# Group norm behind a scan: an earlier bonus load, gate products among the gains, scale and addition in PSUM, four products behind the spreads

## What the reference computes

```python
seq_first = lambda t: jnp.swapaxes(t, 0, 1)
s0 = jnp.zeros((B, H, N, N), f32)
_, y = lax.scan(step, s0, (seq_first(rh), seq_first(wh), seq_first(kh),
                           seq_first(vh), seq_first(kk), seq_first(bh)))
y = jnp.swapaxes(y, 0, 1)
mean = jnp.mean(y, axis=-1, keepdims=True)
var = jnp.mean(jnp.square(y - mean), axis=-1, keepdims=True)
y = ((y - mean) * lax.rsqrt(var + GN_EPS) * ln_w.reshape(H, N).astype(f32)
     + ln_b.reshape(H, N).astype(f32))
bonus = jnp.sum(rh * kh * r_k.astype(f32), axis=-1, keepdims=True) * vh
y = (y + bonus).reshape(B, S, RW_WIDTH).astype(h.dtype)
return (y * jax.nn.silu(gate)) @ w_out
```

## Time and profile before

| | us |
|---|---|
| median of 3 runs (lowest, highest) | 1218.44 (1214.68, 1219.96) |
| profiled execution, its own time | 1217.13 |
| its span, first to last instruction | 1215.3 |
| TensorE busy | 1155.3 (95%) |
| VectorE busy | 742.9 (61%) |
| ScalarE busy | 616.6 (51%) |
| GpSimd busy | 460.8 (38%) |

### The profile page before, as it was taken

How to read it: one execution, slowest core, us unless ns; L and a number is a source line. 1 busy time by engine, 2 the same in 40 slices (tenths; PEclk the granted TensorE clock), 3 DMA queues, 4 the chain that set the end, 5 groups by cost and what they waited for, 6 DMA issues and landing times.

```text
span 1215.3 us, 19475 instructions
## 1 busy us (share of the span) xinstructions
PE 1155.3 (95%) x7562; PEld 891.6 (73%) x7562; DVE 742.9 (61%) x1184; ACT 616.6 (51%) x1028; POOL 460.8 (38%) x375
## 2 busy tenths in 40 slices
PE   6999999989987999899999989999999999999997
PEld 5656777768955777677777767787888888777666
DVE  7758997846666345666676473472394234567764
ACT  6766546425753456455665554452212344566655
POOL 1431023456722444332333334443454445432321
PEclk9998999999998999899999999999999999999988
DMA  9812436253072443222222123432333333321111
GB/s 299 235 52 61 105 86 217 88 161 81 11 262 76 149 131 87 69 59 64 70 70 69 54 71 91 153 103 70 102 89 104 90 101 97 93 71 53 52 35 70
DMA packets 199373, 121.59 MB, mean 100 GB/s; under 512 B 27821, under 2 KB 187254, under 8 KB 198902
## 3 DMA queue, kind: packets, MB, share of 16 engines
q1 hardware_dynamic: 196822, 118.09, 33.2%
q10 hardware_dynamic: 2464, 2.29, 0.6%
HBM read 104.11 MB, written 16.25 MB: 99 GB/s over the span
## 4 chain that ended last, share of the span: by engine, by line
PE 44%; issue 29%; POOL 13%; DVE 9%; ACT 2%; DMA 1%; SPq 0%; POOLq 0%; ACTq 0%; DVEq 0%
POOL b_w_lo L612 13%; PE banks L695 11%; PE banks L697 11%; PE banks L696 11%; PE banks L702 1%; PE banks L1290 1%; PE banks L943 1%; DVE b_suffix L2681 1%; PE banks L1318 1%; DVE b_a_lo L2055 1%; DVE b_w_lo L2165 1%; PE banks L962 1%; PE banks L1300 1%; PE banks L1009 1%; PE banks L1034 1%
## 5 line engine op out<-in xcount | busy, mean ns | idle before, releaser
L612 POOL TENSOR_TENSOR b_w_lo<-b_w_raw,b_w_hi 128x512 fp32r<-128x512 f32 x304 | 404.7, 1353 | 705.8 <-ACT b_w_hi L1388 705.7
L695 PE MATMUL banks<-b_a_lo,b_w_hi 128*128 128x512 f32 x1264 | 517.7, 410 | 23.8 <-DVE b_a_lo L2336 10.5
L697 PE MATMUL banks<-b_a_hi,b_w_lo 128*128 128x512 f32 x1264 | 498.6, 394 | 0.0
L696 PE MATMUL banks<-b_a_hi,b_w_hi 128*128 128x512 f32 x1264 | 497.3, 393 | 0.0
L695 PEld LDWEIGHTS banks<-b_a_lo,b_w_hi 128*128 128x128 f32 x1264 | 240.3, 190 | 103.0 <-issue 21.4
L1388 ACT ACTIVATE b_w_hi<-b_w_raw 128x1024 fp32r<-128x1024 f32 x160 | 168.9, 1056 | 252.0 <-PE banks L697 240.7
L697 PEld LDWEIGHTS banks<-b_a_hi,b_w_lo 128*128 128x128 f32 x1264 | 240.0, 190 | 52.8
L696 PEld LDWEIGHTS banks<-b_a_hi,b_w_hi 128*128 128x128 f32 x1264 | 240.9, 191 | 43.9
L1804 ACT ACTIVATE b_exps<-banks,b_stats 128x128 f32<-128x128 f32 (+3 forms) x64 | 33.2, 524 | 61.1 <-DVE b_stats L2471 61.1
L1720 ACT ACTIVATE b_a_hi<-b_x_t,b_params 128x512 fp32r<-128x512 f32 x48 | 33.9, 718 | 54.7 <-DVE b_x_t L2344 54.2
L2344 DVE TENSOR_TENSOR b_x_t<-b_x_t,banks 128x512 f32<-128x512 f32 x32 | 22.0, 686 | 60.8 <-PE banks L697 60.8
(11 more groups left out here) (330 smaller groups left out, 1520.4 us busy)
## 6 DMA issues: line engine op xcount, KB each, us to landing
b_w_raw<-rw_w_in SPq DMA_DIRECT2D x32, 512.0 KB, 4.4
b_w_raw<-da_w_in SPq DMA_DIRECT2D x32, 512.0 KB, 4.1
b_w_raw<-w_in_a SPq DMA_DIRECT2D x32, 512.0 KB, 4.0
b_w_raw<-pe_w_gate SPq DMA_DIRECT2D x16, 512.0 KB, 4.1
d_ple<-b_ple_out SPq DMA_DIRECT2D x16, 256.0 KB, 3.4
b_w_raw<-rw_w_out SPq DMA_DIRECT2D x8, 512.0 KB, 4.1
b_ple_in<-d_ple SPq DMA_DIRECT2D x2, 2048.0 KB, 11.3
b_w_raw<-da_w_out SPq DMA_DIRECT2D x8, 512.0 KB, 3.9
```

What stands on the lines that cost most here:

```text
L612: m = pool.tensor_tensor(WLO[:, u % 2, ks], WRAW[:, u, ks], WHI[:, u % 2, ks].bitcast(F32), ALU.subtract)
L695: pe.matmul(dst, hi, a_lo[:, k_act, :], start=first, stop=False)
L696: pe.matmul(dst, hi, a_hi[:, k_act, :], start=False, stop=False)
L697: return pe.matmul(dst, lo, a_hi[:, k_act, :], start=False, stop=last)
```

## The change

- The bonus tiles' load moves ahead of the load of x, and the tiles lie where the squares lay, and the other way round (the new place is free once the load of L545 may start). The spread table's load stays where it is.
- The first four head sums move behind the last centring.
- Embeddings 4 and 5 move, with 6 and 7, behind the spreads: embedding j ahead of spread j for j from 4 on. Spreads 4 to 7 wait for the low part j - 4 (`act_ready`), since the bank now holds the value until then.
- ScalarE rounds the spread table ahead of its wait for the head sums; its copies of embeddings and weights are moved to fit.
- VectorE makes gate products 0, 1 and 2 behind gains 1, 3 and 5, with the wait for `gn_in` (both loads) behind gain 1; 3 to 5 ahead of the combination, 6 behind it, 7 in the loop.
- Scale and addition write the spread's bank; ScalarE and VectorE split from there.

```diff
-    BVT, SPREADH2, SPREADHR2, RK2, RKS2, RKC2 = phase([
-        ("bonus_v", [P, NT, TOK]), ("spread_heads2", [P, 2, P]), ("spread_heads2_r", [P, 2, P], F32R),
+    GSQ, SPREADH2, SPREADHR2, RK2, RKS2, RKC2 = phase([
+        ("gn_squares", [P, NT, TOK]), ("spread_heads2", [P, 2, P]), ("spread_heads2_r", [P, 2, P], F32R),
         ("gn_rstd", [P, TOK]), ("gn_signed", [P, TOK], F32R), ("gn_parts", [P, TOK], F32R)])
-    (GSQ,) = phase([("gn_squares", [P, NT, TOK])], 2 * FULL)
+    (BVT,) = phase([("bonus_v", [P, NT, TOK])], 2 * FULL)
...
         sp.dma_start(P1[:, :, :, :].bitcast(F32), D_P1).then_inc(sem("p_spilled"), 16)
+        sp.dma_start(BVT[:, :, :], D_BV.rearrange("j p t -> p j t")).then_inc(sem("gn_in"), 16)
         sp.wait_ge(sem("v_placed"), 2 * 2 * NC)
         sp.dma_start(XT[:, :, :], D_XT.rearrange("j p t -> p j t")).then_inc(sem("x_spilled"), 16)
         sp.wait_ge(sem("y_even"), 2 * NC)
         sp.wait_ge(sem("y_odd"), 2 * NC)
-        sp.dma_start(BVT[:, :, :], D_BV.rearrange("j p t -> p j t")).then_inc(sem("gn_in"), 16)
         sp.dma_start(SPREADH2[:, :, :], a["spread_heads"]).then_inc(sem("gn_in"), 16)
...
             if j == NT - 1:
-                gn_sums(0)
                 pe.wait_ge(sem("gn_kept"), 1)
...
-        gn_sums(1)
+        for b in range(2):
+            gn_sums(b)
         pe.wait_ge(sem("gn_kept"), NT)
-        for n in range(2, 6):
-            second_embedding(n)
+        second_embedding(2)
+        second_embedding(3)
         pe.wait_ge(sem("gn_rstd"), 2)
         for j in range(NT):
-            if j >= 6:
+            if j >= 4:
+
                 second_embedding(j)
-            if j >= 4:
-                pe.wait_ge(sem("gn_scaled"), j - 3)
+                pe.wait_ge(sem("act_ready"), A_RWO + j - 3)
             head_spread(BANK[4 + j % 4], SPREADHR2, RKC2, j).then_inc(sem("gn_bcast"), 1)
...
+        act.wait_ge(sem("gn_in"), 32)
+        act.activation(SPREADHR2[:, :, :], SPREADH2[:, :, :], ACT.Copy)
         act.wait_ge(sem("gn_mm"), 2)
...
-        act.wait_ge(sem("gn_in"), 32)
-        act.activation(SPREADHR2[:, :, :], SPREADH2[:, :, :], ACT.Copy)
...
         keep_second(2)
+        hi(RUN_RWO[0])
         keep_second(3)
-        hi(RUN_RWO[0])
-        keep_second(4)
-        keep_second(5)
         for k in range(NT):
             act.wait_ge(sem("gn_done"), k + 1)
-            split(0, k, YT[:, k, :])
-            if k == 1:
-                keep_second(6)
-            if k == 2:
-                keep_second(7)
+            split(0, k, BANK[4 + k % 4])
+            if k < 4:
+                keep_second(4 + k)
+            if k == 4:
                 hi(RUN_RWO[0] + 1)
...
             stt(out=YT[:, j, :], in0=gn_bank(j), scalar=prm(LN_W, j), in1=GT[:, j, :], op0=ALU.mult, op1=ALU.mult
                 ).then_inc(sem("gn_kept"), 1)
-
-        def gated_bonus(j):
-            own.step(stt(out=BVT[:, j, :], in0=BVT[:, j, :], scalar=prm(LN_B, j), in1=GT[:, j, :], op0=ALU.add, op1=ALU.mult))
+            if j == 1:
+                dve.wait_ge(sem("gn_in"), 32)
+            if j in (1, 3, 5):
+                gated_bonus(j // 2)
...
-            tt(YT[:, j, :], YT[:, j, :], BANK[4 + j % 4], ALU.mult).then_inc(sem("gn_scaled"), 1)
+            tt(BANK[4 + j % 4], YT[:, j, :], BANK[4 + j % 4], ALU.mult).then_inc(sem("gn_scaled"), 1)
...
-            tt(YT[:, j, :], YT[:, j, :], BVT[:, j, :], ALU.add).then_inc(sem("gn_done"), 1)
-
-        dve.wait_ge(sem("gn_in"), 32)
-        for j in range(4):
+            tt(BANK[4 + j % 4], BANK[4 + j % 4], BVT[:, j, :], ALU.add).then_inc(sem("gn_done"), 1)
+
+        for j in range(3, 6):
             gated_bonus(j)
...
+        gated_bonus(6)
         gn_scale(0)
         gn_scale(1)
         gn_add(0)
         for k in range(NT):
-            if k + 4 < NT:
-                gated_bonus(k + 4)
+            if k == 0:
+                gated_bonus(7)
...
-            split_lo(A_RWO, 0, k, YT[:, k, :])
+            split_lo(A_RWO, 0, k, BANK[4 + k % 4])
```

More of the change, by code:

```diff
@@ L2306, in _, with gated_bonus @@
             dve.tensor_copy(P1OUT[:, n, :], BANK[SECOND_BANKS[n]]).then_inc(sem("bank_free"), 1)
+        def gated_bonus(j):
+            own.step(stt(out=BVT[:, j, :], in0=BVT[:, j, :], scalar=prm(LN_B, j), in1=GT[:, j, :], op0=ALU.add, op1=ALU.mult))
         for j in range(NT):
```

## The result

The changed kernel took 1222.9 us, median of 12 runs (1220.0 to 1225.7), beside 1218.6 for the kernel before in as many (1214.7 to 1222.1). The ratio is 1.0039, with a 95% interval of 1.0027 to 1.0051: 4.8 us slower by the ratio, 4.3 by the two medians. The forecast was 0.6 faster, 1217.8, with a range that ended at 1221.5.

A forecast was written before the change was run, and what follows sets the result against it. VectorE's gapless 19.93 us chain holds up slot 0 of the output projection, then TensorE and weights bound. First scale 363.9 plus chain 16.6 gives 380.5, slot 1 at 381.1 against 381.69: 0.6 us faster, 1217.8, range 1210.5 to 1221.5.

The forecast's parts named there:

- Head sums and the copy (1): Ahead of VectorE's combination: sums behind the last centring gain about 0.8 us, the moved table copy 0.3; combination allowed at 355.1.
- gate products (2): On VectorE, products 0 to 2 between gains and 3 to 5 ahead of the combination; with data there, it ends at 356.15.
- The wait (3): VectorE waits behind its second gain, from 346.8, for the spread table landing at 351.5; combination ends 360.9, before 357.0.
- Embeddings at 1.2 GHz (4): TensorE ahead of the spreads: two embeddings fewer save 2.8 us, but the twelve matmuls take 5.3; first scale at 363.9.
- The bank (5): Scale and addition in the bank cost up to 0.4 us more by the records, 0.2 counted; spread 4's wait hidden.
- The collision of gate product 7 (6): In VectorE's chain, GpSimd's subtraction for slot 36 falls on this product, +1.0 us; chain 16.6 against 19.93.
- Embeddings behind spreads, "hidden at 2.4 GHz" (7): TensorE during the chain: embeddings 4 to 7, 1.4 us plus 0.3 per spread, hidden in each period of 1.8.
- Rival D: TensorE idles 3 us between embedding 4 and low part 0, clock falls to 1.2 GHz: 1.9 us slower, 1220.3; chance 0.15.
- B: The spread table lands by 346.8, so VectorE doesn't wait: slot 1 at 374.0, 7.7 us faster, 1210.7; chance 0.18.
- C: The spread table lands at 349.2 and the clock doesn't drop: slot 1 at 376.4, 5.3 us faster, 1213.1; chance 0.12.

The follow-up runs named there:

- run 1: Changed kernel with a semaphore of its own for the bonus load, so VectorE doesn't wait for the spread table behind gain 1; 0.9995 of the kernel before.
- run 5: Changed kernel with the edit of run 1 and embedding 5 made ahead of spread 4, 6 and 7 one place earlier; 0.9932 of the kernel before.
- run 7: The kernel of run 4, but with scale and addition writing SBUF instead of the bank; 0.9971 of the kernel before.
- run 2: Changed kernel, wait for the table kept, with useless matmuls: six ahead of embedding 2, three behind embedding 4; 1.0010 of the kernel before.
- run 3: Changed kernel with the wait for both loads and gate products 0 to 2 moved behind the eight gains; 1.0015 of the kernel before.
- run 6: Changed kernel with the edit of run 1 and TensorE's earlier order, embeddings 2 to 5 ahead of the spreads; 0.9992 of the kernel before.
- run 8: Changed kernel, both loads still on one semaphore, with the load of x issued behind the spread table's; 0.9990 of the kernel before.
- run 9: Changed kernel, its one semaphore and the wait for the table kept, with embedding 5 made ahead of spread 4; 1.0006 of the kernel before.
- run 10: The kernel of run 5 with the bonus load back behind the scan's last output, ahead of the table's; 1.0000 of the kernel before.
- run 4: Changed kernel with the edit of run 1 and three useless matmuls behind embedding 4; 0.9942 of the kernel before.

## Why the prediction was wrong, point by point

- *Head sums and the copy (1), gate products (2)*: right where nothing stands in their way. In run 1 the combination ends at +12.63; the prediction had 356.15, which is +12.61.
- *The wait (3)*: right in mechanism and size; the 351.5 was a choice within 351.4 to 353.0, and the size leans on it. The table was to land at 351.5, +8.0; product 0 started at +7.97. The gains were to end at +14.4 and ended at +14.38, the combination at +17.4 and ended at +17.40.
- *Embeddings at 1.2 GHz (4)*: right in kind. First scale +20.4 predicted, +19.9 measured, since the clock came back for the last few of the twelve.
- *The bank (5)*: no measurable cost; the chain of run 5 is 15.39. And by run 7 a gain of 3.6 us, which the prediction counted only in part, as the 2.1 of collisions of before, less 1.0 for the one that it left in.
- *The collision of gate product 7 (6)*: +1.0 forecast, none in this profile (0.74): it started at 369.57, just as GpSimd went from its first instruction to its second (about 369.7), and it was GpSimd's pair that took longer, 2.96 instead of 2.52. In run 2 it came (1.86). The Trainium skill (SBUF — State Buffer, "SBUF: two separate sides") says that whichever starts first has the shared pair for the whole instruction. Run 7's rows agree: GpSimd started at 358.97, the addition at 359.55 took 1.26 instead of 0.68, and GpSimd's pair then took 2.97. In the changed kernel and in run 2 the two starts lie too close to tell which was first.
- *Embeddings behind spreads, "hidden at 2.4 GHz" (7)*: **this is the step that failed.** The condition, the clock at 2.4 GHz, was written beside it and not met. TensorE idled 3.02 us ahead of spread 4, the clock fell at 373.3, and an embedding with its spread took 3.58 us of TensorE's time instead of 1.7 (1.4 and 0.3). The sum took 16.6 for the chain, without a second fall of the clock; it measured 20.16, +3.6. And it took three matmuls behind the last low part; but with spread 7 late, slot 0 began only at 382.98, and its result came 2.76 behind the last low part where about 1.0 was reckoned, +1.8. Less the 0.5 that the first scale was early, that is 4.9, nearly all of the 5.0 between the forecast 0.6 faster and the 4.4 slower in the stage.
- *Rival D* named this very case, from the same idle spell, but at 0.15, and with 1.9 us. Its size fails at "with the clock back after 7.6 us of work": it took nearly 14 us of work here and in run 1. With that number its own paces (spread 7 at 379.3, slot 0's matmuls 0.42 apart to about 383, then 0.234) give slot 1 at about 386.5, nearly 5 slower in place of 1.9; in the stage it was 4.4. Its path, too, was not quite the one seen: no scale waited for its spread; the low parts waited for ScalarE, whose copies waited for TensorE's slow embeddings. By these runs its chance was too low: the clock fell shortly before or behind spread 4 in the changed kernel and in runs 1, 2, 3, 6, 8, 9 and 10, and stayed up in 4, 5 and 7.
- *Rivals B and C* needed the table earlier. No later load finished ahead of an earlier one (349.9, 355.4 and 355.8 in the order of issue), and run 8 shows that the 2 MB ahead of it made the table late: 9.1 us against 3.3. Run 1 stands as B had it, with no wait and an idle spell of 3.07 ahead of spread 4. B priced a fall of the clock there at 2 us; it cost 5.6 in the stage (run 1 against run 4). B's 7.7 us is about what run 4 gives once both causes are gone, 7.1.

So the change holds three gains (gate products off the chain, the bank, fewer embeddings ahead of the spreads) and two losses that they pay for: a wait for a table that its instruction does not use, and idle spells that drop the clock. With both taken away, the kernel takes 0.9932 of the time of the kernel before (run 5).

## What to carry to other kernels

Give each load a semaphore of its own, or else an early consumer waits for the last landing of all that share it, and a 128 KB load issued behind 2 MB is late by those 2 MB. When work is moved out of TensorE's way to start a chain sooner, look at what TensorE then does while it waits: in runs 1 and 8 and after the change a spell of some 3 us was followed by nearly 14 us at half the clock. In the stage that cost 5.6 us, more than the 2.65 by which two embeddings fewer had brought the first scale forward (run 1 against run 6), and one piece of real work pulled into the spell brought 6.4 back (run 5 against run 1). An operation with two SBUF inputs that meets GpSimd's can be freed of it by keeping one operand in PSUM: 3.6 us in run 7 against run 4.

## What the runs showed of the hardware that I had not expected

- A stretch at 1.2 GHz lasted nearly 14 us (373.3 to 386.9) with TensorE busy in all of it, and as long in run 1; in the kernel before it was some 10 us with idle time in it. It isn't a fixed price: in run 10, also busy without a gap, the clock was 0.52 from 369 to 372 and 0.91 from 372 to 375, so the stretch was over after less than 4 us, and in run 9 after some 7 (0.60 from 370 to 378). What sets its length is open.
- The clock can fall when TensorE is back at work: spread 4 ended the idle spell at 372.29 and the clock fell at 373.3 after the change; in run 1 it was 362.53 and 364.2.
- The length of the idle spell alone does not tell whether the clock falls. Ahead of spread 4, 2.10 us in run 7 and 1.71 in run 5 left it up, while 1.67 in runs 9 and 10 and 1.59 in run 2 were followed by a fall. Ahead of embedding 2, runs 9, 10 and 2 had idled 5.75, 7.05 and 0.68, runs 5 and 7 0.78, which makes no rule; with one profile each, this stays open.
- One instruction more or less of VectorE decides who waits at GpSimd's subtraction: gate product 7 was 0.74 us long after the change, 1.75 in run 7 and 1.86 in run 2.
